# Two plain up panels at the head of each MLP, norm squares on ScalarE, and a wait per bank pair in the down panels

## What is computed

```python
for layer in range(DEPTH):                       # DEPTH = 2
    hn = rms_norm(h, g_mix[layer])
    h = h + attention_mixer(hn, ...)             # layer 0; layer 1: short_conv_mixer(hn, ...)
    h = h + sq_relu_mlp(rms_norm(h, g_mlp[layer]), w_mlp_up[layer], w_mlp_down[layer])

def rms_norm(x, g):
    y = xf * lax.rsqrt(jnp.mean(xf * xf, axis=-1, keepdims=True) + EPS)
    return (y * g)

def sq_relu_mlp(h, w_up, w_down):                # 1024 -> 4096 -> 1024
    return jnp.square(jax.nn.relu(h @ w_up)) @ w_down
```

## Time and profile before

| | us |
|---|---|
| median of 3 runs | 1667.52 (1666.38 to 1669.22) |
| profiled execution, its time | 1666.07 |
| profiled execution, span from first to last instruction | 1664.2 |
| PE busy in the span | 1608.3 |
| DVE, ACT, POOL busy | 1066.7, 719.3, 343.9 |

### The profile page before, as it was taken

One profiled execution on the slowest core, in us unless ns is written; L12 is line 12 of the kernel. 1 busy time (PEld: TensorE's weight loads), 2 busy tenths in 40 slices (PEclk: granted clock), 3 DMA queues, 4 the chain that ended last, 5 costly groups with the idle time before them and its releaser, 6 DMA issues. The chain is left out here.

```text
span 1664.2 us, 29398 instructions
## 1 busy us (share of the span) xinstructions
PE 1608.3 (97%) x12251; PEld 1423.8 (86%) x12251; DVE 1066.7 (64%) x1444; ACT 719.3 (43%) x1132; POOL 343.9 (21%) x270
## 2 busy tenths in 40 slices
PE   8999999989999999999998899999999999989998
PEld 7997777989999999999887788888887788767896
DVE  6544575697666666565569866666657647866644
ACT  5523644454444444221234544444424546575223
POOL 1002212373222222320017322222215100000200
PEclk9999999999999999999999999999999999999999
DMA  6231130213332222222232322223345766201001
GB/s 193 77 82 26 25 87 2 77 51 127 102 102 97 85 99 102 78 76 93 84 101 72 106 101 89 93 99 102 102 97 103 123 83 88 36 1 61 27 28 51
DMA packets 122692, 134.31 MB, mean 81 GB/s; under 512 B 18878, under 2 KB 99509, under 8 KB 122565
## 3 DMA queue, kind: packets, MB, share of 16 engines
q1 hardware_dynamic: 122362, 132.44, 28.5%
q10 hardware_dynamic: 202, 0.06, 0.0%
HBM read 126.13 MB, written 2.10 MB: 77 GB/s over the span
## 5 line engine op out<-in xcount | busy, mean ns | idle before, releaser
L451 ACT ACTIVATE w_hi<-raw 128x1024 fp32r<-128x1024 f32 (+1 forms) x163 | 171.1, 1051 | 417.3 <-PE ps L481 223.1
L1670 PE MATMUL ps<-x_hi,sw_hi 128*128 128x258 f32 (+1 forms) x896 | 256.9, 287 | 16.6 <-DVE x_lo L1563 7.8
L1670 PE MATMUL ps<-x_hi,sw_lo 128*128 128x258 f32 (+1 forms) x896 | 254.4, 284 | 0.0
L1670 PE MATMUL ps<-x_lo,sw_hi 128*128 128x258 f32 (+1 forms) x896 | 254.3, 284 | 0.0
L481 PE MATMUL ps<-x_hi,w_hi 128*128 128x512 f32 (+4 forms) x872 | 246.6, 333 | 2.7 <-DVE x_lo L501 2.6
L481 PE MATMUL ps<-x_lo,w_hi 128*128 128x512 f32 (+4 forms) x872 | 240.3, 326 | 0.0
L481 PE MATMUL ps<-x_hi,w_lo 128*128 128x512 f32 (+4 forms) x872 | 239.8, 326 | 0.0
L458 DVE TENSOR_TENSOR w_lo<-raw,w_hi 128x1024 fp32r<-128x1024 f32 (+1 forms) x163 | 203.5, 1263 | 40.6 <-ACT w_hi L451 40.6
L1711 PE MATMUL ps<-a_hi,w_hi 128*128 128x258 f32 (+1 forms) x768 | 206.3, 323 | 8.5 <-DVE h L1891 8.5
L1711 PE MATMUL ps<-a_hi,w_lo 128*128 128x258 f32 (+1 forms) x768 | 204.9, 321 | 0.0
L1711 PE MATMUL ps<-a_lo,w_hi 128*128 128x258 f32 (+1 forms) x768 | 204.6, 321 | 0.0
(11 more groups left out here) (476 smaller groups left out, 2823.9 us busy)
## 6 DMA issues: line engine op xcount, KB each, us to landing
raw<-in_w_mlp_up SPq DMA_DIRECT2D x32, 1024.0 KB, 5.3
raw<-in_w_mlp_down SPq DMA_DIRECT2D x32, 1024.0 KB, 5.0
raw<-in_w_in SPq DMA_DIRECT2D x16, 1024.0 KB, 9.1
raw<-in_w_in_conv SPq DMA_DIRECT2D x12, 1024.0 KB, 5.0
raw<-in_w_in_attn SPq DMA_DIRECT2D x8, 1024.0 KB, 5.1
raw<-in_w_out_attn SPq DMA_DIRECT2D x4, 1024.0 KB, 5.5
raw<-in_w_out_conv SPq DMA_DIRECT2D x4, 1024.0 KB, 5.3
raw<-in_w_out SPq DMA_DIRECT2D x4, 1024.0 KB, 5.0
```

What stands on the lines that cost most here:

```text
L451: act.activation(split_tile(w_hi, t), raw_tile(t), ACT.Copy).then_inc(w_hi_ok, 1)
L1670: ins = pe.matmul(bank, a[:, w, :], b[:, k, i, 0:hw], start=(k == 0 and j == 0 and m in (1, 2, 7, 5)), stop=(k == 3 and j == 2), skip_grou ...
```

## The change

The first two up panels of each MLP (`PLAIN = 2`) are computed like dense tiles, four tiles in all, from the split chunks `x_hi` and `x_lo` that `norm_act` and `norm_dve` make in the out-projection. The other 14 take the seven products as before; four of the seven operands are mixed rows in a new buffer `xm_hi`, `xm_lo`, and three are read from `x_hi` and `x_lo`. Mixed rows of chunk pairs 0 and 1 are made in the out-projection, those of pairs 2 and 3 in the step of up panel 0. POOL makes no weight sums for the first two panels. A norm's squares are made by ACT (`norm_square`), and POOL only adds them up. The sum over partitions runs in the second tile of panel 0, behind two steps. In the down panels each half waits for the take of the half that used its bank pair last. `take_half` and `norm_dve` change places in DVE's order, and `norm_act`, `norm_square` and `split_hi` in ACT's. The buffers `s1` to `s75` lie where the second model's tables will go, so SP loads those tables only behind the products of the last up panel.

```diff
...
-        def norm_pool_chunk(pool, nm, c):
...
-            dst = acc if c == 0 else sq
-            pool.tensor_tensor(dst[:, f:], h[:, c, f:], h[:, c, f:], ALU.mult).then_inc(sq_ok, 1)
...
+        def norm_square(act, nm, c):
             f, n = nm.first, nm.n - 1
             if c == 0:
-                pool.wait_ge(stat_ok, nm.n)
...
+                act.wait_ge(stat_ok, nm.n)
+            if c >= 3:
+                act.wait_ge(acc_ok, (KC - 1) * n + c - 2)
+            dst = sq_of[c % 2] if c else acc
+            act.activation(dst[:, f:], h[:, c, f:], ACT.Square).then_inc(sq_ok, 1)
+
+        def norm_pool(pool, nm):
...
+            for c in range(1, KC):
+                pool.wait_ge(sq_ok, KC * n + c + 1)
+                pool.tensor_tensor(acc[:, f:], acc[:, f:], sq_of[c % 2][:, f:], ALU.add).then_inc(acc_ok, 1)
                 pool.wait_ge(acc_ok, (KC - 1) * n + c)
...
+        def mix_made(act, nm, i):
...
+            if i or layer:
+                act.wait_ge(xs["lo"], 4 * layer + i)
+            for x in range(2):
+                j = 2 * i + x
+                act.activation(x_f[:, 2 * x:2 * x + 2, 0:hw], h[:, j, f:].rearrange("p (a b) -> p a b", a=2), ACT.Copy,
+                               scale=col(*nm.gain(j))).then_inc(xs["made"], 1)
+
+        def mix_dve(dve, nm, i):
...
+            dve.wait_ge(xs["made"], KC * layer + 2 * i + 2)
+            dve.tensor_tensor(r2, r2, r0, ALU.subtract).then_inc(xs["mixed"], 1)
+            dve.wait_ge(xs["mixed"], n + 1)
+            dve.tensor_tensor(r0, r1, r0, ALU.subtract).then_inc(xs["mixed"], 1)
+            dve.wait_ge(xs["mixed"], n + 2)
+            dve.scalar_tensor_tensor(r1, r2, -1.0, r1, ALU.mult, ALU.subtract).then_inc(xs["mixed"], 1)
+            dve.wait_ge(xs["mixed"], n + 3)
+            dve.scalar_tensor_tensor(r3, r1, -1.0, r3, ALU.mult, ALU.subtract).then_inc(xs["mixed"], 1)
+
+        def mix_hi(act, nm, i):
...
+            act.wait_ge(xs["mixed"], 16 * layer + 4 * i + 4)
+            act.activation(xm_hi[:, i, :, 0:hw], x_f[:, :, 0:hw], ACT.Copy).then_inc(xs["hi"], 1)
+
+        def mix_lo(dve, nm, i):
...
+            dve.wait_ge(xs["hi"], 4 * layer + i + 1)
+            dve.tensor_tensor(xm_lo[:, i, :, 0:hw], x_f[:, :, 0:hw], xm_hi[:, i, :, 0:hw].bitcast(F32), ALU.subtract).then_inc(xs["lo"], 1)
+
+        def out_proj_act(act, t0, nxt):
             for j in range(8):
...
+                split_hi(act, t0 + j + 2)
+                norm_act(act, nxt, j)
+                norm_square(act, nxt, j)
+                if j in (4, 6):
+                    mix_hi(act, nxt, j // 2 - 2)
+                if j in (3, 5):
+                    mix_made(act, nxt, j // 2 - 1)
+
+        def out_proj_dve(dve, t0, nxt):
             for j in range(8):
                 add_dve_tile(dve, t0 + j, j, nxt.first, nxt.width)
...
+                split_lo(dve, t0 + j + 2)
+                norm_dve(dve, nxt, j)
+                if j in (4, 6):
+                    mix_lo(dve, nxt, j // 2 - 2)
+                if j in (3, 5):
+                    mix_dve(dve, nxt, j // 2 - 1)
...
+        def plain_up_pe(pe, nm, layer, u):
+            for y in range(2):
+                t = up_tile(layer, u) + y
+                pe.wait_ge(w_lo_ok, t + 1)
+                if u == 0:
+                    pe.wait_ge(evicted, t - 1)
+                elif y:
+                    pe.wait_ge(scale_ok, nm.n + 1)
+                for k in range(KC):
+                    if u == 0 and y == 0:
+                        pe.wait_ge(x_lo_ok, KC * nm.n + k + 1)
+                    if u == 0 and y == 1 and k == 2:
+                        norm_pe(pe, nm)
+                    for j, (a, b) in enumerate(((w_hi, x_hi), (w_hi, x_lo), (w_lo, x_hi))):
...
+                ins.then_inc(mm_done, 1)
...
                 if y == 0:
                     pe.wait_ge(a_lo_ok, FF // P * layer + 4 * (i // 2 + 1))
-                    pe.wait_ge(evicted, mlp_tile(MLP_T0[layer], "down", i - 1) + 2 if i else MLP_T0[layer] + 2)
                 for x in range(2):
-                    if y and x == 0:
-                        pe.wait_ge(half_in, 2 * n + 1)
-                    if y and x == 1:
-                        pe.wait_ge(evicted, t)
+                    if x == 0 and (i or y):
+                        pe.wait_ge(half_in, 2 * n + y)
+                    if x == 1 and (i or y):
+                        pe.wait_ge(evicted, t if y else mlp_tile(MLP_T0[layer], "down", i - 1) + 2)
+                    if i == 0 and y == 0:
+                        pe.wait_ge(evicted, up_tile(layer, 1) + x + 1)
...
         def up_act(act, nm, layer, u):
+            t = up_tile(layer, u)
             if u == 0:
...
+                mix_made(act, nm, 2)
+                mix_hi(act, nm, 2)
+                split_hi(act, t + 2)
                 norm_scale(act, nm)
                 square_act(act, nm, layer, 0, 0)
+                mix_made(act, nm, 3)
+                split_hi(act, t + 3)
+                mix_hi(act, nm, 3)
                 square_act(act, nm, layer, 0, 1)
...
             elif u == 1:
...
+                prep_act(act, layer, 2, 0)
                 prep_act(act, layer, 2, 2)
...
+                square_act(act, nm, layer, 1, 0)
                 prep_act(act, layer, 2, 3)
...
+                prep_act(act, layer, 2, 1)
                 square_act(act, nm, layer, 1, 1)
...
             for y in range(2):
+                c = 4 * (i % 2) + 2 * y
+                if i >= NU - 2:
+                    norm_act(act, nxt, c)
+                    norm_square(act, nxt, c)
+                    norm_act(act, nxt, c + 1)
                 split_hi(act, t + 2 + y)
                 if i >= NU - 2:
-                    for x in range(2):
-                        norm_act(act, nxt, 4 * (i % 2) + 2 * y + x)
+                    norm_square(act, nxt, c + 1)
...
+        def plain_take(dve, nm, layer, u, y):
...
+            dve.wait_ge(mm_done, t + 1)
...
+            dve.scalar_tensor_tensor(like(tmp[:, y, 0:w], w), in_psum(plain_banks(MLP_T0[layer], u, y), w), 0.0,
+                                     like(scale_bc[:, nm.first:], w), ALU.max, ALU.mult).then_inc(evicted, 1)
...
             if u == 0:
...
+                t = up_tile(layer, 0)
+                mix_dve(dve, nm, 2)
+                mix_lo(dve, nm, 2)
+                dve.wait_ge(scale_ok, nm.n + 1)
+                plain_take(dve, nm, layer, 0, 0)
+                split_lo(dve, t + 2)
                 a_low(dve, nm, layer, 0, 0)
+                mix_dve(dve, nm, 3)
+                plain_take(dve, nm, layer, 0, 1)
+                split_lo(dve, t + 3)
+                mix_lo(dve, nm, 3)
                 a_low(dve, nm, layer, 0, 1)
...
             if u < NU:
+                take_half(0, 0)
                 prep_dve(dve, layer, u, 0)
-                take_half(0, 0)
+                take_half(0, 1)
                 prep_dve(dve, layer, u, 2)
-                take_half(0, 1)
                 prep_dve(dve, layer, u, 3)
+                take_half(1, 0)
                 prep_dve(dve, layer, u, 1)
-                take_half(1, 0)
                 take_half(1, 1)
                 return
             for y in range(2):
+                c = 4 * (i % 2) + 2 * y
                 take_half(y, 0)
+                if i >= NU - 2:
+                    norm_dve(dve, nxt, c)
                 take_half(y, 1)
+                if i >= NU - 2:
+                    norm_dve(dve, nxt, c + 1)
                 split_lo(dve, t0 + 2 + y)
...
             mlp_load(sp, 1)
-            sp.wait_ge(fx["out_lo"], 8)
+            sp.wait_ge(evicted, mlp_tile(T_MLP1, "up", NU - 1) + 2)
             load_second_tables(sp)
...
```

More of the change, by code:

```diff
@@ L1535, in sums_pool @@
             pool.tensor_tensor(dst, a, b, ALU.add).then_inc(summed, 1)
[L1537 to L1547, removed]
-                act.activation(x7_hi[:, i, 0:2, 0:hw], x_f[:, 1:3, 0:hw], ACT.Copy).then_inc(x_hi_ok, 1)
-            else:
-                act.wait_ge(xs["made"], KC * layer + j + 1)
-                act.activation(x7_hi[:, i, 2:4, 0:hw], x_f[:, 3:5, 0:hw], ACT.Copy).then_inc(xs["hi"], 1)
-                act.wait_ge(xs["mixed"], 16 * layer + 4 * i + 4)
-                act.activation(x7_hi[:, i, 4:7, 0:hw], x_f[:, 5:8, 0:hw], ACT.Copy).then_inc(x_hi_ok, 1)
@@ L1618, in mlp_pool @@
         def mlp_pool(pool, nm, layer):
[L1619 to L1627 removed]
+            norm_pool(pool, nm)
+            for u in range(PLAIN, NU):
@@ new lines, in product_pe @@
+        def product_pe(pe, nm, layer, u, m):
+            n, t, hw = nth_up(layer, u), up_tile(layer, u), nm.width // 2
+            first = u == PLAIN
+            bank = ps[:, P_BANK[m], 0:hw]
+            if m == 1:
+                pe.wait_ge(w_lo_ok, t + 1)
+                if first:
+                    pe.wait_ge(evicted, MLP_T0[layer] + 2)
+                else:
+                    pe.wait_ge(copied, 3 * n)
+            if m == 5:
+                pe.wait_ge(p_lo, 2 * n + 1)
```

(22 more changed lines are left out.)

258 lines of the change are left out of this document (70 added, 188 removed).

## The result

The kernel after takes 1629.14 us (median of 4 runs, 1628.01 to 1630.15); the kernel before, beside it, 1667.93. The profiled execution took 1630.15 with a span of 1628.4.

A forecast was written before the change was run, and what follows sets the result against it. PE was taken as full mid-MLP, losing time only at each MLP's head and end; gains of 10.0 + 9.1 (heads) and 3.4 + 2.7 (ends) gave 25.2 us, from 1667.5 to 1642, range 1634 to 1654.

The forecast's parts named there:

- The order of the takes in the middle ... where PE is full: 0: Middle of each MLP: reordering DVE's takes is off PE's path, since PE is busy throughout; gain 0.
- 1.0 and 1.4 for down 0's second tile: Heads: wait left for the first half's take, 1.0 us in layer 0 (from 2.08), 1.4 in layer 1.
- The other waits left at the head: Panel 1's second tile, panel 2's product copy, the scale: 0.9, 0.4, 0 us in layer 0; 1.4, 0.8, 0.5 in layer 1.
- The move of the squares to ACT costs nothing: Heads: ACT waits for PE there and PE for no square, so the move costs 0.
- a down panel's first half now waits for the half that used its bank pair: Last three down panels: that half is taken 2.9 us earlier, so losses of 2.4 and 2.0 us go.
- The norm stretch's 1.05 and 0.71: Start of the next projection: idles of 1.05 and 0.71 us go, as DVE runs `norm_dve` ahead of `split_lo`.
- The rows show the clock low only behind 3.73 and 2.08: Kernel before: low clock only behind those two head idles (us); used to give the clock-swing rule 0.06 of 0.16.
- rival of half rate: Heads and ends: short waits add up or the clock falls behind one; gain only 13.6 us, 1654; chance 0.16.
- the price of the plain panels: Heads: two panels per layer go from 84 to 96 matmuls, costing 2.9 us in layer 0, 1.8 in layer 1.
- the norm sum's 0.7: Heads: the sum over partitions still costs PE 0.7 us in each layer.
- SP at 0: Second model's table and weight loads, now behind the last up panel: 13.8 us of cover, so cost 0.
- The rival called clean: Heads and ends: POOL runs beside DVE, only the sum over partitions is left; gain 31.9 us, 1635.6; chance 0.13.

The follow-up runs named there:

- late sums: The kernel after, with POOL's weight sums for panel 2 held back until panel 0's first half tile is taken: 1633.42 us, ratio 0.9776.
- old head: The kernel before, plus the wait per bank pair, takes first and the new end order; squares on POOL, first panels mixed: 1662.19 us, ratio 0.9947.
- squares alone: The kernel before, with only the squares of the norms behind the down phases moved to ACT: 1665.5 us, ratio 0.9976.
- old end order: The kernel after, with ACT's and DVE's old order in the last two down panels, squares still on ACT: 1630.01 us, ratio 0.9771.
- old head with the squares: The old head's kernel, with the squares of the norms behind the down phases also on ACT: 1649.41 us, ratio 0.9882.
- old take order: The kernel after, with DVE's takes behind two mixed rows again in down panels 0 to 11: 1638.1 us, ratio 0.9812.
- end squares on POOL: The kernel after, with the squares of the norms behind the down phases back on POOL: 1638.08 us, ratio 0.981.

## Why the prediction was off

The direction and most mechanisms held; the size didn't, by 12.8 us, and that came from four terms.

**"The order of the takes in the middle ... where PE is full: 0"** is the step that failed worst: the old order costs 5.4 us. Part of it is the head. I followed the new order and still took 1.0 and 1.4 for down 0's second tile; the rows show 0 and 0.33 with it, and 1.02 and 1.59 with the old one, which is what my working really priced. The other part is the middle of layer 1. A stretch with PE busy for 20.00 of 20.00 us was read as a full one, but a down panel of layer 1 took 11.31, and the prediction's own spacing, 48 times 0.2273, gives 10.91. That spacing was too small, since the 88 of the earlier trace rows also counts matmuls cut by the window's edges. From start to start in the same stretch of the kernel before there are 85 steps:

```profile
840.10 0.39 PE L481 MATMUL ps<-x_hi,w_lo 128*128 128x512 f32 x1
...
859.80 0.39 PE L481 MATMUL ps<-a_hi,w_hi 128*128 128x512 f32 x1
```

So the spacing is 19.70 / 85 = 0.2318 and a full panel 11.13, which is after's 11.12. The 0.2 lost before lies at the second tile's first matmul, which needs the take of the first half. PE's and DVE's timelines of the kernel before, in the panel from 963.66 to 974.97:

```profile
969.01 0.40 PE L1711 MATMUL ps<-a_hi,w_lo 128*128 128x512 f32 x1
969.36 0.47 PE L1711 MATMUL ps<-a_hi,w_hi 128*128 128x512 f32 x1
...
968.53 0.68 DVE L1891 TENSOR_TENSOR h<-h,ps 128x512 f32<-128x512 f32 x1
```

The take ends at 969.21, and the matmul starts 0.35 behind the one before it and the next one 0.31 behind it; no bracket marks this, because the row ahead of it lasts 0.40. In after the take of the panel from 956.33 ends at 960.55, and the same step is 0.26.

**The other waits left at the head**, 0.9 + 0.4 + 0 and 1.4 + 0.8 + 0.5, came to idles of 0 and 0.43, and by the starts of the matmuls, which also show what no bracket marks, to 0.3 and 0.85. I had the chain to panel 1's second split end 16.9 us behind the out-projection without POOL and 19.4 with it. In layer 1 it ends at 18.2 (896.77 + 1.22 - 879.77), and in the run with late sums at 16.2 (894.61 + 1.22 - 879.60): both a little early, and the lock worth 2.0 instead of 2.5. With down 0's take, and less 0.4 for the plain panels of layer 1, it makes the heads 4.7 better than forecast.

**"The move of the squares to ACT costs nothing"**, true, and mis-sized as a gain. The lock of DVE behind POOL was worked out for the head, from the earlier trace rows, and not for the ends, where it lengthens DVE's work for half a panel from 5.8 to 7.4 us. The last panels came out at 4.8 for a forecast of 4.4, but for half the reason: "a down panel's first half now waits for the half that used its bank pair" gives nothing by itself (old head: 37.10), the squares alone next to nothing (36.96 for 37.01), and both together 34.75. The norm stretch's 1.05 and 0.71 were 3.59 and 1.19, and with the squares on ACT the order that I credited gives 0.1 and 0.2 (old end order: 7.98 and 7.64); the squares have nearly all of it. In layer 0 a second idle of 0.47 and the low clock behind it belong to the same term: both are gone with the squares alone.

**"The rows show the clock low only behind 3.73 and 2.08"** was wrong about the kernel before: it was low behind 1.05 and 0.47 too. The rival of half rate named the Trainium skill's rule (TensorE: Matmul & The Clock Gate, section "A second HAM failure mode: psum-queue depth-cycling") that small pauses can make the clock swing. The trace of before agrees in this place; after has no such run of pauses, and its clock is 1.00 in both heads.

**Right:** the price of the plain panels in layer 0 (in layer 1 they take 11.12 for 10.91, so 0.4 more in all), no idle at up panel 0's first step, the norm sum's 0.7, SP at 0, and no wait in the second model's tiles. The head rows stand at 45.8 and 45.6 for 48.1 and 47.9. The rival called clean (1635.6) had the head of layer 0 nearly right (12.6), that of layer 1 1.7 too high (13.2), and lies 6.5 us above the result, above all for the middle and the norm stretches, which it priced like the forecast. Its reason, POOL beside DVE and not in front, doesn't hold: late sums show POOL in front of DVE at 2.0 us in layer 1.

**Open:** an up panel in the middle takes 10.05 and 9.94 in after, 10.10 and 10.00 to 10.02 in before, in the old head and in the old head with the squares. Over 13 panels this is 0.7 and some 0.9 us of the middle's gain. It comes with the new heads, which also read three of the operands from another buffer; no run took that apart.

## What to carry to other kernels

Compare a panel's measured length with its matmul count times the spacing of an undisturbed stretch before calling PE full, and take the spacing from starts, not from a window's count: busy digits hide losses of 0.2 us a panel. When one engine's operation lengthens another's, price it at every place where the two meet, and test two edits for the same wait together as well as alone, since either can hide the other. Moving one item forward in a chain without room can bring its wait back behind it, as both moves at the head did here.

## What the runs showed of the hardware

The granted clock can fall in code that an edit doesn't touch. Stretches of the run with the old take order:

```profile
1565.00:1570.00 5.00, 4.72 (x79) 4.49 (x77) 1.22 (x4) 1.30 (x4) 0.00 (x0) 0.82 0.00 0
1570.00:1575.00 5.00, 5.00 (x39) 4.66 (x39) 1.93 (x5) 0.00 (x0) 0.00 (x0) 0.50 0.01 3
1575.00:1580.00 5.00, 5.00 (x32) 5.00 (x32) 0.92 (x2) 1.26 (x3) 0.00 (x0) 0.66 0.61 193
```

The three stretches add up to some 10 us at half rate, 5 x (0.18 + 0.50 + 0.34) / 0.5, with PE busy for 14.72 of 15. From the norm sum of layer 1 to the end that execution takes 1636.3 - 1232.21 = 404.1 us against 1628.4 - 1228.77 = 399.6 in after. Single idles of 1.02 and 1.59 (old take order) and of 1.26 and 1.24 (end squares on POOL) left it at 1.00 in the 5 us behind them, while 1.05 and 0.47 close together did not. In the kernel before, 2.08 in layer 0 was followed by 0.66 in the next 5 us and 2.28 at the same place of layer 1 (948.05) by 1.00, so the length of one idle doesn't decide it. What does was not tried.
